# Where a chunked scan inverts its first blocks: in the projections' tail and in steps 0 and 1

## The reference

```
cb, cc, cx, r, k, v, w_lo, a_lo, g_lo = split_proj(h @ w_in)
kk    = normalize(k * k_k)                     # per head of 64
decay = exp(-DECAY_SCALE * sigmoid(w0 + tanh(w_lo) @ w_up)); a = sigmoid(a0 + a_lo @ a_up)
S = S * decay - (S kk) (kk * a)^T + v k_d^T    # per token, per head, both directions
y = S r
y_conv = cb * shortconv1d(cc * cx, conv_a_w)
```

## Time and profile before

| what | us |
|---|---|
| median of 3 runs (range) | 2296.94 (2296.35 to 2301.68) |
| the profiled execution: span from first to last instruction | 2289.2 |
| PE busy in the span | 2074.5 (91%) |
| DVE busy | 1526.2 (67%) |
| ACT busy | 874.0 (38%) |
| POOL busy | 779.6 (34%) |

### The profile page before, as it was taken

The page is one execution under the profiler, slowest core; times in us unless marked ns, Lnnn a source line. Parts: engine busy times, 40 slices in busy tenths (PEclk is TensorE's granted clock), DMA queues, the critical chain, the costliest instruction groups (busy, mean ns, idle before and its releaser), DMA issues. The chain is left out here.

```text
span 2289.2 us, 36974 instructions
## 1 busy us (share of the span) xinstructions
PE 2074.5 (91%) x15096; PEld 1597.3 (70%) x15096; DVE 1526.2 (67%) x2035; ACT 874.0 (38%) x1411; POOL 779.6 (34%) x456
## 2 busy tenths in 40 slices
PE   7779999936888898999999989999899999999898
PEld 1657777735777676788877767887676777776566
DVE  5887667679785447888888890346636675545644
ACT  3444444413443446433333341343424443333320
POOL 0434334300020042877777743534222101111111
PEclk9889999976899999999999999999999999999999
DMA  7563343478674512122222265424211111102512
GB/s 287 189 204 121 109 134 113 136 217 217 182 206 135 185 47 92 47 83 83 83 83 83 73 231 171 162 90 127 74 67 65 58 45 47 65 19 74 193 55 83
DMA packets 181335, 271.16 MB, mean 118 GB/s; under 512 B 74280, under 2 KB 122024, under 8 KB 176816
## 3 DMA queue, kind: packets, MB, share of 16 engines
q1 hardware_dynamic: 176560, 252.02, 33.9%
q10 hardware_dynamic: 4608, 16.78, 2.0%
HBM read 200.53 MB, written 68.23 MB: 117 GB/s over the span
## 5 line engine op out<-in xcount | busy, mean ns | idle before, releaser
L105 PE MATMUL b_ps<-h_hi,b_wpool 128*128 128x512 f32 (+1 forms) x976 | 300.4, 385 | 19.2 <-issue 7.4
L2961 PE MATMUL g_ps<-g_h_hi,w 128*128 128x512 f32 x784 | 258.2, 401 | 4.9 <-ACT g_q L3154 4.9
L3274 POOL TENSOR_TENSOR w<-raw_down,w 128x1024 fp32r<-128x1024 f32 x38 | 94.1, 2475 | 459.9 <-ACT w L3132 459.9
L105 PEld LDWEIGHTS b_ps<-h_hi,b_wpool 128*128 128x128 f32 x976 | 182.7, 192 | 67.2 <-issue 18.7
L2230 DVE SCALAR_TENSOR_TENSOR e_vars<-grid,vec,e_vars 128x1024 f32<-128x1024 f32 x168 | 216.1, 1286 | 7.5 <-ACT e_vars L1977 4.2
L105 PE MATMUL b_ps<-h_lo,b_wpool 128*128 128x512 f32 (+1 forms) x488 | 184.7, 379 | 0.0
L2961 PEld LDWEIGHTS g_ps<-g_h_hi,w 128*128 128x128 f32 x784 | 147.6, 188 | 39.1 <-ACT g_q L3154 5.6
L2961 PE MATMUL g_ps<-g_h_lo,w 128*128 128x512 f32 x392 | 154.6, 394 | 0.0
L2642 POOL TENSOR_TENSOR g_down_lo<-raw_down,g_down_hi 128x1408 fp32r<-128x1408 f32 x26 | 86.7, 3338 | 141.7 <-ACT g_down_hi L2542 141.7
L2481 PE MATMUL g_pb<-g_z_hi,g_down_hi 128*128 128x512 f32 x286 | 114.7, 401 | 14.8 <-DVE g_down_lo L2719 9.8
L717 POOL TENSOR_TENSOR b_wpool<-raw_in,b_wpool 128x1024 fp32r<-128x1024 f32 x26 | 67.9, 2612 | 169.9 <-ACT b_wpool L515 169.9
(11 more groups left out here) (511 smaller groups left out, 5305.0 us busy)
## 6 DMA issues: line engine op xcount, KB each, us to landing
e_raw_up<-w_ffn SPq DMA_DIRECT2D x22, 1024.0 KB, 4.8
raw_down<-w_down SPq DMA_DIRECT2D x32, 704.0 KB, 4.1
c_op<-ops SPq DMA_DIRECT2D x40, 512.0 KB, 5.0
raw_down<-w SPq DMA_DIRECT2D x38, 512.0 KB, 3.7
b_xin<-ada_rows ACTq DMA_DIRECT2D x32, 512.0 KB, 5.3
raw_in<-w SPq DMA_DIRECT2D x26, 512.0 KB, 4.2
zs<-e_z SPq DMA_DIRECT2D x21, 512.0 KB, 2.6
ops<-b_xin SPq DMA_DIRECT2D x20, 512.0 KB, 5.1
```

The costliest lines, as they stand in the source:

```text
L105: last = nc.tensor.matmul(out, w[:, k, :], x[:, k, cols], start=(k == 0 and n == 0), stop=(k == nk - 1 and n == 2))
L2961: mm = nc.tensor.matmul(out_bank, ww[w % 2][:, k], xx[g][:, k], start=(k == 0 and a == 0), stop=(k == KD - 1 and a == 2))
L3274: nc.gpsimd.tensor_tensor(w_lo[w % 2], raw[:, w % 2], w_hi[w % 2].bitcast(F32), ALU.subtract).then_inc(sem("lo"), 1)
```

## The change

- **Where the blocks are made.** The four `scan_blocks` move from between the last `cx` and `cb` products into the last turn of the loop, between `r` and the second `cb` product. They now write four PSUM banks instead of two, and ACT's four copies stand before its `hi` of `cx`.
- **SP in the last turn and the tail.** The operand loads for `scan_blocks` come right after `cc`'s weights; then `store_vt`, `cx`'s weights, the 16 stores of raw blocks, the store of the convolution, the load of the blocks for the inversion, and only then `cb`'s weights. The last store of the convolution signals a semaphore that outlives the block, and SP waits for it in step 10 of the scan.
- **DVE in the tail.** The inversion is now a class `Inverse` (same instructions), with buffers that outlive both blocks (`inverse_n`, `inverse_u`, `inverse_t`, `inverse_w`). Part 0 (`small`) stands after `normed(3, 1)`, part 1 (`eights`) after `products(3, 3)`, part 2 (`inner` and `outer("low")`) after `products(3, 4)`.
- **The scan's start.** DVE does part 3 of batch 0 and goes on to the triangles. ACT starts four operand loads and six of the twelve loads of the inverse on its own queue. Pairs 4 and 5 are multiplied in steps 0 and 1. The memsets are on POOL (those of the inversion's buffers at the kernel's start).
- **The steps.** DVE does parts 0 and 1 of batch 1 in step 0, parts 2 and 3 in step 1, parts 0 and 1 of batch 2 in step 2, part 2 in step 3, part 3 in step 4, and from step 5 on what it did before. The inverses of batch 1 are stored and loaded in step 2 instead of 1.
- The buffer set aside for descriptors (`dynamic_dma_scratch_size`) is set to 1024.

The core of the diff:

```diff
-        block_bank = (ps[PS_HEADS], ps[PS_NORM])
+        block_bank = ((ps[PS_W], ps[PS_A]), (ps[PS_HEADS], ps[PS_NORM]))
+        inverse_bufs = t["inverse"]
+        mul = tmp[:, 5:7].rearrange("p a c -> p (a c)")[:, 0:2048]
...
                 load_w(("cc", c + 1))
-                load_w(("v", n + 1) if n + 1 < PAIRS else ("cx", n))
-                store_vt(n)
-                store_conv(c)
+                if n + 1 < PAIRS:
+                    load_w(("v", n + 1))
+                    store_vt(n)
+                    store_conv(c)
             m = PAIRS - 1
-            load_w(("cb", m))
             sp.wait_ge(sem("chunk"), chunk[("k", m, 0)] + 1)
...
-            store_job(m, 2)
-            store_bonus(m)
-            store_job(m, 3)
-            store_job(m, 4)
+            store_vt(m)
+            load_w(("cx", m))
             for i in range(2):
                 for x in range(2):
                     sp.wait_ge(sem(f"raw_blocks{x}"), i + 1)
                     for h in range(2):
                         for b in range(2):
                             sp.dma_start(d["pb"][0, x, h, b, 2 * PAIRS * i:2 * PAIRS * (i + 1)].rearrange("n r c -> r n c"),
+            store_conv(m - 1)
+            sp.wait_ge(sem("pb"), 256)
+            sp.dma_start(inverse_bufs[0][:, 0:HB * HB], d["pb"][0].rearrange("x h b n r c -> (x h b n) (r c)")).then_inc(sem("nb"), 16)
+            load_w(("cb", m))
+            store_job(m, 2)
+            store_bonus(m)
+            store_job(m, 3)
+            store_job(m, 4)
             store_job(m, 5)
-            store_conv(m)
-            sp.wait_ge(sem("pb"), 256)
+            store_conv(m, t["ahead"]("mixd"))
-            sp.wait_ge(sem("conv_stored"), 16 * PAIRS)
+            sp.wait_ge(sem("conv_stored"), 16 * (PAIRS - 1))
...
-                pe.wait_ge(sem("bonus"), 2 * PAIRS)
-                if i:
-                    pe.wait_ge(sem(f"raw_blocks{x}"), i)
+                if i == 0:
+                    pe.wait_ge(sem("tanh"), job(PAIRS - 1, 1))
+                elif x == 0:
+                    pe.wait_ge(sem("vt"), PAIRS * 3)
+                else:
+                    pe.wait_ge(sem("norm"), (PAIRS - 1) * 3 + 1)
                 src = pre[x][i].rearrange("p (j q) (a c) -> p j q a c", j=2, a=2)
-                out = block_bank[x][:].rearrange("p (j q c) -> p j q c", j=2, q=PAIRS)
+                out = block_bank[i][x][:].rearrange("p (j q c) -> p j q c", j=2, q=PAIRS)
...
                 dense("r", n, 2)
+                if n == PAIRS - 1:
+                    for i in range(2):
+                        for x in range(2):
+                            scan_blocks(x, i)
                 dense("cb", c, 2)
...
-            for x in range(2):
-                scan_blocks(x, 0)
             dense("cb", c, 1)
-            for x in range(2):
-                scan_blocks(x, 1)
             dense("cb", c, 2)
...
+                if n == PAIRS - 1:
+                    for i in range(2):
+                        for x in range(2):
+                            act.wait_ge(sem(f"p_blocks{x}"), i + 1)
+                            A(pre[x][i][:, :, 0:C], block_bank[i][x][:].rearrange("p (n c) -> p n c", c=C),
+                              ACT.Copy).then_inc(sem(f"raw_blocks{x}"), 1)
                 hi(*(("v", n + 1) if n + 1 < PAIRS else ("cx", n)))
...
+            nc.gpsimd.memset(inverse_bufs[2], 0.0).then_inc(sem("ui_clear"), 1)
...
             sums(m, 2)
             normed(m, 1)
+            dve.wait_ge(sem("ui_clear"), 3)
+            dve.wait_ge(sem("nb"), 16)
+            dve.wait_ge(sem("vt_stored"), 128 * PAIRS)
+            inverse.small()
             sums(m, 3)
             products(m, 2)
             normed(m, 2)
             bonus(m)
             sums(m, 4)
             products(m, 3)
+            inverse.eights()
             conv_in(c, 1)
             sums(m, 5)
             products(m, 4)
+            dve.wait_ge(sem("bonus_stored"), 16 * PAIRS)
+            inverse.inner()
+            inverse.outer("low")
             conv_in(c, 2)
...
+        pres.update({0: 4, 1: 5})
+        parts = {0: ((1, 0), (1, 1)), 1: ((1, 2), (1, 3)), 2: ((2, 0), (2, 1)), 3: ((2, 2),), 4: ((2, 3),)}
+        parts.update({s: (((s + 7) // BATCH, (s + 7) % BATCH),) for s in range(5, 13)})
+        stores = {s: (s + 3) // BATCH for s in range(5, STEPS) if (s + 3) % BATCH == 0 and s + 3 < STEPS}
+        stores[2] = 1
...
-                if s == 0:
-                    store_raw(2)
-                if s == 1:
-                    load_blocks(2)
                 if s - 1 in pres and pres[s - 1] % 2:
                     load_blocks(pres[s - 1] // 2)
-                if (s + 3) % BATCH == 0 and s + 3 < STEPS:
-                    store_blocks((s + 3) // BATCH)
-                    load_inverse((s + 3) // BATCH)
+                if s in stores:
+                    if s == 2:
+                        sp.wait_ge(sem("clear1"), 1)
+                    store_blocks(stores[s])
+                    load_inverse(stores[s])
...
-            load_blocks(0)
             for x in DIRS:
                 load(x, 0)
-            load_pre(2)
-            load_pre(3)
+            store_blocks(0)
+            sp.wait_ge(sem("clear"), 1)
+            sp.wait_ge(sem("ub"), 16)
+            inverse_diag(sp, 0, 0)
+            sp.wait_ge(sem("tb"), 16)
+            inverse_level(sp, 0, 0)
             for x in DIRS:
                 load(x, 1)
             for h in HEADS:
                 sp.dma_start(t["pend"][ROWS[h], 1, NCTX:SLOTS], d["pends"][ROWS[1 - h]]).then_inc(sem("pend"), 16)
+            store_raw(1)
+            load_blocks(1)
             load_pre(4)
             load_pre(5)
-            store_raw(1)
-            load_blocks(1)
-            sp.wait_ge(sem("clear"), 1)
-            store_blocks(0)
-            load_inverse(0)
-            load_pre(6)
-            load_pre(7)
             for s in range(STEPS):
                 step(s)
...
-            for i in (2, 3, 4, 5):
+            for i in (2, 3):
                 blocks(i)
             for x in DIRS:
-                wait("raw", x, 4)
...
+            for i in (2, 3):
+                for x in DIRS:
+                    pre_from(act, x, i)
             both_dirs(token_major, 0)
-            for i in (2, 3, 4, 5):
+            act.wait_ge(sem("ub"), 16)
+            inverse_level(act, 0, 1)
+            act.wait_ge(sem("clear"), 1)
+            act.wait_ge(sem("tb"), 16)
+            inverse_diag(act, 0, 1)
+            for i in (2, 3):
                 both_dirs(blocks, i)
...
-            nc.vector.memset(ui[:, 0:HB * HB:HB + 1], 1.0).then_inc(sem("ui_clear"), 1)```

On DVE, in the tail between the normalization of keys 1 (ends at `b_tmp<-b_tmp,b_rstd`) and the scan of decays of job 3. Before:

```order
L844 RECIPROCAL b_rstd<-b_rstd 128x512
L846 TENSOR_TENSOR b_tmp<-b_tmp,b_rstd 128x512
L807 SCALAR_TENSOR_TENSOR b_xin<-con_mixer,b_xin 128x512
L808 TENSOR_SCALAR b_xin<-b_xin,vec,b_ka 128x512
L814 TENSOR_TENSOR b_xin<-b_xin,b_tmp 128x512
```

244 lines of the change are left out of this document (135 added, 109 removed).

## The result

The changed kernel took 2308.01 us (median of 6 runs, 2303.61 to 2312.01), the kernel before, run beside it, 2298.28 (6 runs). The ratio is 1.0058, with a 95% interval of 1.0040 to 1.0077: slower, by 9 to 18 us. The forecast was 2302, with "slower" at 0.35.

The account below looks back on a forecast made before the run. The prediction took both places that exchange work, tail and scan's start, to be bound by DVE or round trips. Its terms, +13.6 - 23.7 + 15.3 = +5.2 on 2296.94, gave 2302 us, range 2287 to 2311.

Parts of the forecast that it names:

- Term 1(b): Tail, up to job 3's scan: stores, blocks' load, part 0 and ACT's wait for `cb`'s weights delay that scan by +9.4.
- Term 1(a): Tail: `cx`'s weights, issued behind the vts stores, land later and delay ACT's `tanhs(3, 2)` by +4.3.
- Terms 1(c) and (d): End of tail: `eights` +3.8, `inner` and `outer("low")` +7.3; then `pends` and the block's end, scan's start at 498.4, +13.6.
- Term 2: Scan's start to first state update: 5.2 MB must move, 17.8 us at 292 GB/s; update after 29.5 instead of 53.2, -23.7.
- The high bound: Scan's start to first update: 33.9 us (-19.3) if step 1's operands, 1.3 MB more, must land too.
- Term 3: Update 0 to update 5: moved inversion parts and a wait of 4 in step 2 make 82.6 instead of 67.3, +15.3.
- the 7.7 between span and median: Whole kernel: the median was taken to lie 7.7 us above the profiled span.
- signs of being right: Scan's start near 498; DVE idle before part 0 and job 3's scan; update 28 to 31 later; intervals 18, 16, 21; `ub` wait.
- signs of being wrong: Scan's start below 494; first update under 27 us later; no wait in step 2; step 5's shift not the end's.
- the queues and their round trips decide: Rival, scan's start and step 2: transfers wait in line, first inverse at high bound; +13.8, 2310 us; chance 0.25.

Follow-up runs that it names:

- x2: Changed kernel with the low part of `cb`'s weights computed on DVE behind part 0 instead of on POOL: ratio 1.0046.
- w3: Changed kernel with the inversion's four buffers at the other end of the memory, plus the edits of x2 and x3: ratio 1.0024.
- x3: Changed kernel with the four `scan_blocks` behind the last `cb` product and `cx`'s weights issued ahead of the vts stores: ratio 1.0041.
- z3: Changed kernel with ACT's four operand loads of pairs 2 and 3 behind its share of the inverse's pieces: one run, 2318.14 us.
- z1: Changed kernel with only the first half: batch 0's three parts stay in the tail, batch 1's first two return ahead of step 0: ratio 1.0111.
- x1: Changed kernel with all four parts of batch 0's inversion back at the scan's start: ratio 1.0053.
- x4: Changed kernel with the operand loads of pairs 2 and 3 on SP's queue, ahead of the inverse's store, instead of on ACT's: ratio 1.0065.

## Why the prediction was wrong

The mechanisms were named rightly, the balance was not. It said that the tail loses, the start wins and steps 0 to 2 lose again, and all three did. It missed by 6 us of median; the terms by 10.4, and the median came nearer than the terms only because not all of their +15.6 is seen in the time, which is luck.

- **Term 1(b) failed**, in the sentence that a POOL operation would cost "about 0.6 ..., since ACT's path hides most of it". Part 0 took 4.2 more than 7.3 (11.5), and ACT hid none: job 3's scan began without any idle time, directly behind part 0. The prediction counted one of three POOL operations; L844, which follows DVE's own L962, and L834, which follows ACT's L673, stood there as well. With one taken away (x2, w3) part 0 took 8.4 and 8.3. The path was wrong too. (b) had DVE wait for the blocks and then for ACT behind `cb`'s weights, +9.4; the trace has neither wait. Job 2's scan came 6.3 later behind K, part 0 added 11.5, and the 4.74 of idle time was filled: +12.9 for job 3's scan.
- Term 1(a) was forecast as +4.3. Between K and `tanhs(3, 2)` it was 11.2 after and 5.8 before: +5.4, and the second `conv_out` moved by as much (10.2 and 4.7). x3 gave back 1.5 of it at S. Terms 1(c) and (d) held: job 5's scan came 4.0 later against job 3's (forecast +3.8), DVE's end another 7.2 later (+7.3), and S 4.5 behind DVE's end (forecast 3.9).
- **Term 2 failed**, in the step "at 292 GB/s that is 17.8 us". The level came at S + 21.8. The rate was about right and the sum of bytes too small: 6.1 MB moved by then, at 280 GB/s, where it had counted 5.2, as SP issues step 1's operands (from 523.73 on) before the last pieces have landed. At 292 GB/s they would have taken 20.9; the rest is a slower start, 227 GB/s in the 4.7 us ahead of the inverse's store. Seen as a chain the same time is the store, 4.7 behind S, which shares the engines with the pairs' loads and lands after 7.1, and its pieces, 4.7 to 5.4. z3 measured the store at 3.3 without these loads and the last piece at S + 14.1, so the chain alone was not the limit; how much is the chain under load and how much the bytes no run tells apart. From the level to the update it took 12.6 instead of 11.75. The high bound, S + 33.9 to the first update, was about right (34.4), and it was the one with step 1's operands.
- Term 3 was right in its parts: steps of 20.0, 16.3 and 21.6 (18.1, 16.3 and 21.1 expected), with a wait of 4.4 for the store in step 2 (4). Step 0 was 1.9 dearer, and steps 3 and 4 took 25.9 instead of 27.1.
- K's shift had no term, and the 7.7 between span and median was taken as fixed. Neither is the cause of the miss in the terms.
- Of its own signs of being right, two failed and two held: DVE was not idle ahead of part 0 or of job 3's scan, the first update came 34.4 behind S and not 28 to 31; the steps near 18, 16 and 21 and the wait in step 2 came. None of its signs of being wrong clearly came, so they were set too wide.
- The rival that came true is "the queues and their round trips decide", 2310, from "the inverse reaches PE later than S + 20". It had 0.25. It was priced with the wrong sum: the tail lost more, step 2 less.

Behind these lies one omission. The prediction asked how soon batch 0 could be ready and not what the second batch's blocks do meanwhile. z1 shows that they arrive 32 to 33 us after S anyway, so before the change DVE's inversion at the start was partly free, by the very wait that the change was to use.

The trace supports the rule that the prediction cited, the Trainium skill, "SBUF — State Buffer", section "Who interferes with whom": a pair of products of 0.29 whose second ends just behind POOL's 2.34 operation, and 8.4 instead of 11.5 when that operation is gone. What failed was how often it was applied.

## What to carry to other kernels

Before work is moved out of a busy stretch, ask what other chain, of transfers above all, ran beside it: if that chain is as long, the stretch doesn't get shorter, and the moved work is added where it goes. List every GpSimd operation that can fall beside a row of short VectorE products with two inputs, and price each at up to its whole length. Price a store and load again of the same data twice, as a chain of landings under the load of that moment and as all the bytes that move until its end, those queued behind it too.

## What the runs showed of the hardware

- Three two-input products of DVE, about 0.2 us long alone, ended 0.04 to 0.07 us behind the GpSimd operation that ran beside them (changed); the operations were 1.27, 2.34 and 1.06 long.
- A store of 512 KB took 2.6 to 4.1 us from issue to landing when the queues were light (x1, z3, before), and 6.2 to 8.1 beside four loads of 512 KB (changed, x4, z1); pieces of 64 KB took 2.4 to 3.2 in the same three and, in the changed kernel, 4.7 to 5.4 (medians by tile).
- The same kernel, before, took from 2285 to 2307 us in one measurement of 29 runs. The mean granted clock ran against it: in five such measurements it was 0.954 to 0.962 in the quickest run and 0.949 to 0.954 in the slowest, and a least-squares line through all runs gives 12 to 15 us per 0.01. One profile's span can thus differ by 10 us for no reason in the code. Three profiles of the kernel before have spans of 2289.2, 2290.2 and 2304.1, and update 5 at 186.7 to 188.8 behind K: most of the scatter lies behind update 5, and differences between landmarks within one trace are what can be compared.
